# Recurrence of a linear-attention block: products of one chunk with the two decayed streams as 128 stationary columns

## What is computed

```python
def step(S, inp):
    r_t, w_t, k_t, v_t, kk_t, a_t = inp
    sa = jnp.einsum('bhvk,bhk->bhv', S, kk_t)
    S = (S * w_t[:, :, None, :]
         - sa[..., None] * (kk_t * a_t)[:, :, None, :]
         + v_t[..., None] * k_t[:, :, None, :])
    y = jnp.einsum('bhvk,bhk->bhv', S, r_t)
    return S, y
```

## Time and profile before

| what | value |
|---|---|
| median of 3 runs | 2397.78 us (2395.69 to 2399.03) |
| profiled execution | 2396.95 us, of which span 2395.2 us |
| mean granted clock of TensorE | 0.998 |
| TensorE busy | 98% of the span |
| chain that ended last | PE 92%, DVE 5%, ACT 2%, issue 1% |
| recurrence on TensorE | from 454.30 us, last copy of Y ends at 525.54 us |

### The profile page before, as it was taken

How to read it: one execution, slowest core, us unless ns; L and a number is a source line. 1 busy time by engine, 2 the same in 40 slices (tenths; PEclk the granted TensorE clock), 3 DMA queues, 4 the chain that set the end, 5 groups by cost and what they waited for, 6 DMA issues and landing times.

```text
span 2395.2 us, 48279 instructions
## 1 busy us (share of the span) xinstructions
PE 2357.9 (98%) x19991; PEld 2202.7 (92%) x19991; DVE 1543.8 (64%) x1901; ACT 1207.7 (50%) x1590; POOL 17.1 (1%) x36
## 2 busy tenths in 40 slices
PE   9999999989999999999999999999999999999998
PEld 9999799879998899999999999999999888888886
DVE  8588588566774455657799875656755444565445
ACT  5586563354464466754644346465545333444343
POOL 0000000000000000000000000000000000000000
PEclk9999999999999999999999999999999999999999
DMA  9355565325555655564566565554665555665564
GB/s 285 116 185 175 178 191 187 102 74 179 182 168 187 187 153 159 178 203 141 159 193 179 166 185 166 186 178 150 198 198 175 192 185 188 189 185 183 193 186 148
DMA packets 216554, 419.88 MB, mean 175 GB/s; under 512 B 17057, under 2 KB 19441, under 8 KB 215649
## 3 DMA queue, kind: packets, MB, share of 16 engines
q1 hardware_dynamic: 207520, 397.98, 52.6%
q0 software_dynamic: 2560, 10.59, 1.4%
q10 hardware_dynamic: 6288, 8.61, 1.3%
HBM read 410.84 MB, written 6.29 MB: 174 GB/s over the span
## 4 chain that ended last, share of the span: by engine, by line
PE 92%; DVE 5%; ACT 2%; issue 1%; DMA 0%; DVEq 0%; ACTq 0%
PE ps L504 26%; PE ps L505 26%; PE ps L506 26%; PE ps L1148 5%; PE ps L1150 3%; DVE wlo L369 1%; PE ps L724 1%; ACT whi L365 1%; PE ps L652 1%; PE ps L638 1%; PE ps L732 0%; PE ps L988 0%; DVE regions L2002 0%; DVE act_parts L2316 0%; PE ps L1003 0%
## 5 line engine op out<-in xcount | busy, mean ns | idle before, releaser
L369 DVE TENSOR_TENSOR wlo<-wraw,whi 128x1024 fp32r<-128x1024 f32 x752 | 916.4, 1224 | 766.7 <-ACT whi L365 765.4
L365 ACT ACTIVATE whi<-wraw 128x1024 fp32r<-128x1024 f32 x752 | 792.5, 1058 | 1017.2 <-PE ps L506 921.4
L504 PE MATMUL ps<-act_parts,whi 128*128 128x256 f32 (+2 forms) x3968 | 1130.9, 285 | 11.5 <-DVE act_parts L2316 7.5
L505 PE MATMUL ps<-act_parts,whi 128*128 128x256 f32 (+2 forms) x3968 | 1117.3, 282 | 0.0
L506 PE MATMUL ps<-act_parts,wlo 128*128 128x256 f32 (+2 forms) x3968 | 1116.1, 281 | 0.0
L504 PEld LDWEIGHTS ps<-act_parts,whi 128*128 128x128 f32 x3968 | 746.4, 188 | 18.9 <-issue 12.6
L505 PEld LDWEIGHTS ps<-act_parts,whi 128*128 128x128 f32 x3968 | 748.7, 189 | 1.0
L506 PEld LDWEIGHTS ps<-act_parts,wlo 128*128 128x128 f32 x3968 | 746.7, 188 | 0.0
L505 PE MATMUL ps<-wlo,regions_r 128*128 128x512 f32 x512 | 202.2, 395 | 0.0
L506 PE MATMUL ps<-whi,regions_r 128*128 128x512 f32 x512 | 202.2, 395 | 0.0
L504 PE MATMUL ps<-whi,regions_r 128*128 128x512 f32 x512 | 202.2, 395 | 0.0
(11 more groups left out here) (377 smaller groups left out, 1650.2 us busy)
## 6 DMA issues: line engine op xcount, KB each, us to landing
wraw<-in_a_w_in SPq DMA_DIRECT2D x128, 512.0 KB, 3.7
wraw<-in_w_up SPq DMA_DIRECT2D x128, 512.0 KB, 3.8
wraw<-in_w_down SPq DMA_DIRECT2D x128, 512.0 KB, 4.4
wraw<-in_w_in SPq DMA_DIRECT2D x112, 512.0 KB, 3.6
wraw<-in_b_w_qg SPq DMA_DIRECT2D x64, 512.0 KB, 3.9
wraw<-in_a_w_out SPq DMA_DIRECT2D x32, 512.0 KB, 3.9
wraw<-in_w_k_shared SPq DMA_DIRECT2D x32, 512.0 KB, 3.7
wraw<-in_w_v_shared SPq DMA_DIRECT2D x32, 512.0 KB, 3.6
```

The source lines that it names most:

```text
L365: nc.scalar.activation(whi[:, q % RING], wraw[:, q % RING], ACT.Copy).then_inc(hi_ready, 1)
L369: nc.vector.tensor_tensor(wlo[:, q % RING], wraw[:, q % RING], whi[:, q % RING].bitcast(F32), ALU.subtract).then_inc(lo_ready, 1)
L504: mm(o, hi_s, hi_m, start=first, stop=False, skip_group_check=True)
L505: mm(o, hi_s, lo_m, start=False, stop=False, skip_group_check=True)
```

## The change

`KR` is laid out as [j, chunk, a, 64], so that for one chunk the two streams are 128 contiguous columns. The state products of an early step become 32 products of 64 rows x 128 stationary columns (W on output partitions 0 to 63, Y on 64 to 127), the value products 16 per half f likewise, all into banks f + 4p. ACT then copies W out of partitions 0 to 63 and Y out of 64 to 127 of two banks each, with two instructions where one stood (L1412, L1422 become L1419, L1430). The early key products and the turns use other banks. The semaphore for the value products and two waits for the state products go; the turn of `Bc` in an early step waits for the copy of Y, the second key half for one Y copy fewer, and the state product for the masks of the second key half. The scan becomes four of 64 elements per j. Of the diff (accesses of `KR` elsewhere only change their pattern):

```diff
-        KR = R[:, 2:4, :].rearrange("p a n -> p (a n)").rearrange("p (j a t) -> p j a t", j=KT, a=2)
+        KR = R[:, 2:4, :].rearrange("p a n -> p (a n)").rearrange("p (j c a t) -> p j c a t", j=KT, c=4, a=2)
...
+        KEY_BANK, TOK_BANK = (((2, 3), (4, 5)), ((2, 3), (0, 4))), ((0, 1), (1, 5))
...
                     elif n_:
-                        pe.wait_ge(S["y_sb"], 2 * it)
+                        pe.wait_ge(S["y_sb"], 2 * it - 1)
...
                 if it < 3:
-                    if not early:
+                    if early:
+                        pe.wait_ge(S["y_sb"], 2 * it)
+                    else:
                         pe.wait_ge(S["am_ready"], 6 * it + 2)
-                    turn(Bc, 0)
+                    turn(Bc, TOK_BANK[early])
                     pe.wait_ge(S["am_ready"], 6 * it + (2 if early else 4))
-                    turn(Kc, 2)
+                    turn(Kc, (2, 3))
                 if early:
+                    pe.wait_ge(S["am_ready"], 6 * it + 4)
                     if it < 3:
                         pe.wait_ge(S["tok_ready"], 4 * it + 2)
-                    into_tokens((0, 1), 0, chan(KR, 0, ts), state, last=False, sig=S["state_mm"], over=1)
-                    state_n += 2
-                    pe.wait_ge(S["state_mm"], state_n)
+                    else:
+                        pe.wait_ge(S["y_sb"], 2 * it)
+                    for i, p in SLOTS:
+                        for f in range(2):
+                            m_ = mm(ps[:, f + 4 * p, cols(i)], KR[side(f), 2 * i + p, it].rearrange("p a t -> p (a t)"), state(f, i, p), start=i == 0, stop=False,
+                                    skip_group_check=True)
+                    m_.then_inc(S["state_mm"], 1)
+                    pe.wait_ge(S["state_mm"], it)
...
                     for i, p in SLOTS:
-                        w_ = mm(ps[side(1 - p), f, cols(i)], am(1)(f, i, p), value(f, i, p), start=i == 0 and not early, stop=it == 0 or early, skip_group_check=True)
-                        y_ = mm(ps[side(p), 4 + f, cols(i)], am(2)(f, i, p), value(f, i, p), start=i == 0, stop=False, skip_group_check=True)
-                    w_.then_inc(S["w_mm"] if early or it == 0 else S["first_mm"], 1)
-                    y_.then_inc(S["first_mm"], 1)
-                    first_n += 1 if early or it == 0 else 2
-                if it:
-                    pe.wait_ge(S["m_sb"], 2 * it)
-                    pe.wait_ge(S["first_mm"], first_n)
-                    if not early:
-                        into_tokens((0, 1), 0, chan(KR, 0, ts), state, first=False, sig=S["w_mm"], over=1)
-                    into_tokens((0, 1), 4, chan(KR, 1, ts), state, first=False, last=False, sig=S["state_mm"])
-                    state_n += 2
+                        m_ = mm(ps[:, f + 4 * p, cols(i)], AM[side(p), 8 * f + i, 1:3, :].rearrange("p a t -> p (a t)"), value(f, i, p), start=i == 0 and not early, stop=False,
+                                skip_group_check=True)
+                    m_.then_inc(S["w_mm"], 1)
...
                 for f in range(2):
                     act.wait_ge(S["w_mm"], 2 * it + f + 1)
-                    st.do(a(Wt[:, f * GW:(f + 1) * GW], bank(f), ACT.Copy), sig["w_sb"])
+                    for p in range(2):
+                        st.do(a(Wt[side(1 - p), f * GW:(f + 1) * GW], ps[side(0), f + 4 * p, :], ACT.Copy), sig["w_sb"] if p else None)
...
-                    st.do(nc.vector.tensor_tensor_scan(KR[:, j, 1, :], cs("restart"), KR[:, j, 0, :], 0.0, ALU.mult, ALU.add),
-                          sig["dec_done"] if j == KT - 1 else None)
+                    for c in range(4):
+                        st.do(nc.vector.tensor_tensor_scan(KR[:, j, c, 1, :], cs("restart")[:, 0:CH], KR[:, j, c, 0, :], 0.0, ALU.mult, ALU.add),
+                              sig["dec_done"] if j == KT - 1 and c == 3 else None)
```

More of the change, by code:

```diff
@@ L211, in program @@
         xk = R[:, 1, :].rearrange("p (k t) -> p k t", k=KT)
-        KR = R[:, 2:4, :].rearrange("p a n -> p (a n)").rearrange("p (j a t) -> p j a t", j=KT, a=2)
+        KR = R[:, 2:4, :].rearrange("p a n -> p (a n)").rearrange("p (j c a t) -> p j c a t", j=KT, c=4, a=2)
+        streams = R[:, 2:4, :].rearrange("p a n -> p (a n)").rearrange("p (x a t) -> p x a t", x=4 * KT, a=2)
+        stream4 = lambda g, a_: streams[:, 16 * g:16 * g + 16, a_, :]
         by_two = lambda t_, n: t_.rearrange("p (i c a t) -> p i c a t", i=n, c=4, a=2)
@@ L766, in level @@
                         pe.wait_ge(S["bcm_ready"], 4)
-                    into_tokens((f,), AB_BANK[c], key(Bc, c), chan(KR, 0, ts), sig=S["ab_mm"], over=1)
+                    into_tokens((f,), AB_BANK[c], key(Bc, c), chan(KR, c, 0), sig=S["ab_mm"], over=1)
                 if kind == "gather":
@@ L814, in _ @@
             pe.wait_ge(S["silu_ready"], 3)
-            first_n = state_n = 0
             for it in range(4):
@@ L832, in _ @@
                 if not early:
-                    into_tokens((0, 1), 0, key(Bc, it), chan(KR, 1, ts), sig=S["am_mm"])
+                    into_tokens((0, 1), 0, key(Bc, it), chan(KR, it, 1), sig=S["am_mm"])
                 for n_ in range(2):
@@ L839, in _ @@
                     elif n_:
-                        pe.wait_ge(S["y_sb"], 2 * it)
+                        pe.wait_ge(S["y_sb"], 2 * it - 1)
                     for i, p in SLOTS[8 * n_:8 * n_ + 8]:
                         for f in range(2):
-                            m_ = mm(ps[side(p), 2 + 2 * n_ + f, (i % 4) * P:(i % 4 + 1) * P].rearrange("p (a t) -> p a t", a=2),
-                                    Kc[side(f), i, it, p, :], KR[side(f), 2 * i + p, :, ts], start=True, stop=True)
+                            m_ = mm(ps[side(p), KEY_BANK[early][n_][f], (i % 4) * P:(i % 4 + 1) * P].rearrange("p (a t) -> p a t", a=2),
+                                    Kc[side(f), i, it, p, :], KR[side(f), 2 * i + p, it], start=True, stop=True)
                             if i % 4 == 3 and p:
@@ L888, in _, with outputs @@
                     within_tokens(f, 2 + f, flat_over(TTs[:, it]), flat_over(Wt)).then_inc(S["u_mm"], 1)
+                def outputs(f):
+                    for i, p in SLOTS:
+                        m_ = mm(ps[side(1), f + 4 * p, cols(i)], am(0)(f, i, p), flat(U)(f, i, p), start=False, stop=True, skip_group_check=True)
+                    m_.then_inc(S["y_mm"], 1)
                 pe.wait_ge(S["u_sb"], 2 * it + 1)
-                if it:
-                    pe.wait_ge(S["state_mm"], state_n)
-                within_tokens(0, 4, am(0), flat(U), first=False).then_inc(S["y_mm"], 1)
+                outputs(0)
                 pe.wait_ge(S["u_sb"], 2 * it + 2)
@@ L895, in _ @@
                     into_channels(6, tok(0), flat(U), first=False, sig=S["m_mm"])
-                within_tokens(1, 5, am(0), flat(U), first=False).then_inc(S["y_mm"], 1)
+                outputs(1)
             def turn_y(j2):
@@ L906, in turn_y @@
                 m_.then_inc(S["zt_mm"], 1)
-            keep_warm(15, 0)
+            keep_warm(15, 2)
             for j2 in range(2):
                 turn_y(j2)
-            keep_warm(7, 0)
+            keep_warm(7, 2)
             def turn_ahead(h):
@@ L1253, in sigmoids @@
                     for j in (2 * j2, 2 * j2 + 1):
-                        st.do(a(chunks(KR[:, j, 0, :]) if i == 0 else tile_of(Bc, j), chunks(ps[:, 4 + n_ % 4, (j % 2) * T:(j % 2 + 1) * T]), ACT.Sigmoid,
+                        st.do(a(KR[:, j, :, 0, :] if i == 0 else tile_of(Bc, j), chunks(ps[:, 4 + n_ % 4, (j % 2) * T:(j % 2 + 1) * T]), ACT.Sigmoid,
                                 bias=ve("w0" if i == 0 else "a0", j)), sig["lora_s1"])
@@ L1271, in _ @@
             act.wait_ge(S["dec_done"], 1)
-            st.do(a(gC[:], KR[:, :, 1, CH - 1::CH], ACT.Exp, scale=-DECAY))
+            st.do(a(gC[:], KR[:, :, :, 1, CH - 1], ACT.Exp, scale=-DECAY))
             def key_part(t):
@@ L1279, in key_part @@
                 j4 = slice(4 * g, 4 * g + 4)
-                cum = KR[:, j4, 1, :]
+                cum = stream4(g, 1)
                 if w == 0:
@@ L1284, in key_part @@
                     for i in range(2):
-                        st.do(a(as_tiles(by_two(tmpA[2], 2)[:, i]), in_tiles(cum[:, 2 * i:2 * i + 2, :]), ACT.Exp, scale=DECAY),
+                        st.do(a(as_tiles(by_two(tmpA[2], 2)[:, i]), KR[:, 4 * g + 2 * i:4 * g + 2 * i + 2, :, 1, :], ACT.Exp, scale=DECAY),
                               sig["kp_act"] if i else None)
                 if w == 1:
-                    st.do(a(KR[:, j4, 0, 1:T], KR[:, j4, 1, 0:T - 1], ACT.Exp, scale=-DECAY), sig["kp_act"])
+                    st.do(a(stream4(g, 0)[:, :, 1:CH], cum[:, :, 0:CH - 1], ACT.Exp, scale=-DECAY), sig["kp_act"])
                 if w == 2:
@@ L1404, in _ @@
                         act.wait_ge(S["m_mm"], 2 * it)
-                    st.do(a(BKt[:, u // 2, 4 * (u % 2):4 * (u % 2) + 4, :], bank(u).rearrange("p (i m) -> p i m", i=4), ACT.Copy), sig["tok_ready"])
```

(6 more changed lines are left out.)

25 lines of the change are left out of this document (13 added, 12 removed).

## The result

The changed kernel takes 2409.48 us (median of 6 runs, 2406.20 to 2413.88) against 2397.66: ratio 1.005, 95% interval 1.004 to 1.006. It is 11.8 us slower, where the forecast was 2399.5 and the range ended at 2406. The six runs form two groups, by the mean granted clock of TensorE: three at 0.996 take 2406.2 to 2406.6, three at 0.992 or 0.993 take 2412.4 to 2413.9.

The account below looks back on a forecast made before the run. TensorE was taken to bound the kernel, its recurrence waiting for code; longer products, copies and form changes less vanished stalls summed to +2.1 us, giving 2399.05 or 2399.9, stated as 2399.5 us, range 2391 to 2406.

Parts of the forecast that it names:

- rival C: TensorE's clock falls in new gaps of steps 1 and 3, perhaps 2; two falls 2403 us, three 2405; chance 0.16.
- "same" band: Measured times of 2393.0 to 2402.6 us, which the measurement cannot tell from no change; chance 0.53.
- Price of the new form: 64x128 products in two row groups on TensorE: 56.5 ns a record, between bounds of 29 and 113.
- A: The load is hidden: 128 stationary columns at the pace of 64, 29 ns a record, 2388 us; chance 0.08.
- B: Row groups take turns on TensorE: 113 ns a record, 25 us more, 2424 us; chance 0.04.
- Value and state products: On TensorE: state +1.46 us a step in steps 1 to 3; values +1.34 in steps 1 and 2, +1.8 in step 0.
- Stalls for code: TensorE's waits for instructions vanish: −1.91 us in step 0, −1.49 in step 1, −1.53 in step 2.
- D: Code still comes late on TensorE: half the stalls stay, +2.5 us, 2402, or 2403.8 with one fall; chance 0.09.
- ACT: W and Y leave PSUM as two copies each: +0.48 us a pair, unhidden for Y in steps 1 and 2.
- Waits: State product's new waits for second-half masks and Y: no cost in steps 1 and 2; masks bind in step 3.
- Changes of form: Five more switches between TensorE product shapes in the four steps: 0.08 us each, 0.4 in all, at most 1.4.
- Scans: Four DVE scans of 64 replace each of 256: +0.6 to +2.4 us per slab, hidden, cost nil, upper end +4.

Follow-up runs that it names:

- e5_light_fill: Changed kernel plus products of constants sized to TensorE's waits: four in step 1, none in step 2, two and four in step 3; 2401.22 us.
- e2_quads: Changed kernel with its layout, banks, waits and copies, but each state and value product as two of 64 columns; 2401.20 us.
- e3_values64: Changed kernel with only the value products as two of 64 columns, the state product keeping 128; 2403.88 us.
- e6_gap64: e2_quads with one wait more in step 2: the state product also waits for ACT's last bonus piece of the step before; 2404.13 us.
- e6_gap128: e5_light_fill with one wait more in step 2: the state product also waits for ACT's last bonus piece of the step before; 2410.87 us.
- e8_before_tokens: Kernel before the change, with ACT's token copies ahead of the bonus pieces and nothing else changed; 2398.05 us.

## Why the prediction was wrong

The step that failed is rival C's price, as the prediction put it: "A fall costs half of the stretch at 1.2 GHz, +1.75 where TensorE is busy all through; my sum holds none. One fall gives 2401.2, still no change". It took the length of the stretch from a kernel whose next products were 64x64 and dense, and kept that length for products of 64x128. A fall lasts 13 us with them and costs 5 to 6 us, so one fall leaves the "same" band and two leave the range. And the sum put falls at none, although the prediction worked out gaps of 1.5 to 2.0 us and knew a fall behind 1.91: the profile has two falls, worth 5.8 and 5.7 us, 11.5 of the 12.5 that the recurrence took beyond the forecast. It had the chance of two falls or more at 0.16, where every run of the changed kernel had a clock that one or two falls explain; both falls of the profile are in steps 1 and 3, where C looked for them, though behind waits shorter than C's 1.5 to 2.0 us.

Point by point:

- *Price of the new form*: right. 56 ns a record forecast; 64 records in 3.72 to 3.81 us at full clock. Rivals A and B fall with it.
- *Value and state products, step by step*: right at full clock (e5_light_fill, within 0.5 us a step).
- *Stalls for code*: nearly right. 0.77 us is left in step 1, none shows in step 2, and step 0 keeps its clock. e2_quads, with as many products as before, has them back. D falls. That they are waits for code is an inference from e2_quads and the queue's count; no run changed the code's delivery alone.
- *ACT*: mis-sized, +0.61 a pair where +0.48 was put: copies of 64 x 512 follow each other at 0.61 us, not at the 0.47 of 128 x 512.
- *Waits*: the masks bind in step 3, as put; M from DVE also binds there (0.69) and in step 2 (0.39), which was left out.
- *Sum*: +2.1 forecast, +2.9 measured at full clock (e5_light_fill against its kernel before), with an interval of 1.0 to 5.5 us, so the 0.8 between them is inside what can be told. In the profile the recurrence takes 2.4 us more (table), where the forecast has 1.75 and its 0.4.
- *Changes of form*: none shows; where nothing is waited for the next form follows at once.
- *Scans*: 16 of 64 take 3.02 us where four of 256 took 2.43, +0.59 a slab, the low end of what was put, and hidden as put: the recurrence starts at 454.25 after and 454.30 before.

Open: why the clock falls behind step 1's waits of 0.77 and 1.07 us and not behind step 2's 0.39 and 1.44, which are as much, and why some runs of the changed kernel have one fall and others two. That 64x128 products behind a wait let it fall where 64x64 would not is suggested by step 1 of e3_values64 and e2_quads, and not proved.

## What to carry to other kernels

Price a fall of TensorE's clock with the products that will come behind it, not with those of the profile at hand: here 64x128 products ran at half speed from the fall to their end, and the clock came back only among the 64x64 products behind them. Before putting fewer, wider products where dense small ones stood, look at each wait ahead of them, and size constant products to that wait, no longer (here 5.8 us over the kernel before with too many, 2.9 with few). The trade of instruction count against loads was worth nothing that the runs can tell here: e2_quads and e5_light_fill are 3.2 and 2.9 us over the kernel before.

## What was not expected of the hardware

- The stretch at 1.2 GHz lasted 3.5 us ahead of 64x64 products before, 6.6 in e6_gap64, 13 in the changed kernel and 17 in e6_gap128. TensorE was busy in 12.9 of the 13 us and stayed at 0.50. The clock came back at 491.8 and 536.2 in the changed kernel and 516.2 in e6_gap128, where the last 64x128 products ended at 487.9, 532.7 and 513.9.
- The length of a wait does not by itself decide the fall. e5_light_fill waits 1.60 us for M in step 2 and stays at 1.00. e8_before_tokens waits 2.6 us at one place (TensorE's wait, us in total, times, longest) and its clock stays at 1.00 over the whole recurrence, by the window under it:

```profile
PE ps L732 <- issue: 2.6, 1, 2.6
```

```profile
454.00:540.00 86.00, 72.30 (x2484) 67.62 (x2483) 55.69 (x101) 49.48 (x115) 3.53 (x5) 1.00 0.22 74
```

- Copies of 64 rows x 512 follow each other at 0.61 us, copies of 128 x 512 at 0.47.
